# A hybrid decoder layer on one Trainium2 core: the openings of its two feed-forward layers put in the order of the block products, and part of the weight split given to GpSimd

## What is computed

```python
def rmsnorm(x, g):
    xf = x.astype(jnp.float32)
    y = xf * lax.rsqrt(jnp.mean(xf * xf, axis=-1, keepdims=True) + EPS)
    return (y * g.astype(jnp.float32)).astype(x.dtype)

def swiglu(x, w_gate, w_up, w_down):
    return (jax.nn.silu(x @ w_gate) * (x @ w_up)) @ w_down

# in trunk_layer
x = x + 0.5 * swiglu(rmsnorm(x, p['g_ffn1']), p['w1_gate'], p['w1_up'], p['w1_down'])
...
x = x + 0.5 * swiglu(rmsnorm(x, p['g_ffn2']), p['w2_gate'], p['w2_up'], p['w2_down'])
```

## Time and profile before

| | us |
|---|---|
| median of 3 runs | 2257.41 |
| the runs | 2261.75, 2255.10, 2257.41 |
| profiled execution, its own time | 2258.11 |
| its span, first to last instruction | 2256.3 |
| TensorE busy | 2173.1 |
| VectorE busy | 1346.7 |
| ScalarE busy | 712.2 |
| GpSimd busy | 399.7 |
| mean granted clock of TensorE, share of full speed | 0.986 |

### The profile page before, as it was taken

One profiled execution on the slowest core, in us unless ns is written; L12 is line 12 of the kernel. 1 busy time (PEld: TensorE's weight loads), 2 busy tenths in 40 slices (PEclk: granted clock), 3 DMA queues, 4 the chain that ended last, 5 costly groups with the idle time before them and its releaser, 6 DMA issues.

```text
span 2256.3 us, 37791 instructions
## 1 busy us (share of the span) xinstructions
PE 2173.1 (96%) x15020; PEld 2024.1 (90%) x15020; DVE 1346.7 (60%) x2013; ACT 712.2 (32%) x1270; POOL 399.7 (18%) x427
## 2 busy tenths in 40 slices
PE   6799999999999999989999999998999999999998
PEld 5799999998989888878898878988999999989897
DVE  7867666664424678899525145358676676644234
ACT  6422322322212415547312034144223223222122
POOL 1000000000000156768634321520000000000003
PEclk9899999999999999999999999999999999999999
DMA  3122112116423211153411162311221221163222
GB/s 138 60 74 95 60 72 95 65 59 236 120 68 91 99 65 38 59 147 101 166 33 35 37 235 82 134 39 58 77 94 58 76 95 59 66 236 120 68 73 79
DMA packets 70861, 206.63 MB, mean 92 GB/s; under 512 B 9703, under 2 KB 31207, under 8 KB 63079
## 3 DMA queue, kind: packets, MB, share of 16 engines
q1 hardware_dynamic: 67808, 201.84, 26.5%
q10 hardware_dynamic: 2951, 3.35, 0.4%
HBM read 161.14 MB, written 41.23 MB: 90 GB/s over the span
## 4 chain that ended last, share of the span: by engine, by line
PE 85%; DVE 9%; DMA 2%; issue 1%; ACT 1%; POOL 1%; SPq 0%; DVEq 0%; ACTq 0%; POOLq 0%
PE ps L799 27%; PE ps L800 26%; PE ps L801 26%; PE ps L1344 1%; PE ps L1385 1%; DMA dn_raw<-in_w_dn 1%; DVE act_lo L1953 1%; DVE x L2001 1%; DVE t_lo L2009 1%; PE ps L1069 1%; DVE rstd L1940 1%; DMA w_raw<-in_w_plain 0%; DVE acc L2170 0%; PE ps L825 0%; DVE st L2426 0%
## 5 line engine op out<-in xcount | busy, mean ns | idle before, releaser
L799 PE MATMUL ps<-act_hi,op_hi 128*128 128x272 f32 x1280 | 369.8, 289 | 11.4 <-DVE op_lo L2030 11.4
L800 PE MATMUL ps<-act_lo,op_hi 128*128 128x272 f32 x1280 | 371.4, 290 | 0.0
L801 PE MATMUL ps<-act_hi,op_lo 128*128 128x272 f32 x1280 | 370.6, 290 | 0.0
L699 POOL TENSOR_TENSOR w_hi<-w_raw,ones 128x256 fp32r<-128x256 f32 x148 | 133.7, 903 | 1052.8 <-DMA w_raw<-in_w_plain 794.8
L799 PE MATMUL ps<-act_hi,w_hi 128*128 128x288 f32 (+1 forms) x864 | 291.1, 337 | 8.9 <-DVE act_lo L1953 4.4
L799 PE MATMUL ps<-hs_hi,dn_hi 128*128 128x288 f32 (+1 forms) x864 | 284.4, 329 | 0.9 <-DVE x L2129 0.8
L801 PE MATMUL ps<-act_hi,w_lo 128*128 128x288 f32 (+1 forms) x864 | 284.7, 329 | 0.0
L800 PE MATMUL ps<-hs_lo,dn_hi 128*128 128x288 f32 (+1 forms) x864 | 282.4, 327 | 0.0
L801 PE MATMUL ps<-hs_hi,dn_lo 128*128 128x288 f32 (+1 forms) x864 | 282.3, 327 | 0.0
L799 PE MATMUL ps<-t_hi,op_hi 128*128 128x272 f32 x960 | 277.0, 289 | 0.0
L801 PE MATMUL ps<-t_hi,op_lo 128*128 128x272 f32 x960 | 277.0, 289 | 0.0
(11 more groups left out here) (332 smaller groups left out, 4230.2 us busy)
## 6 DMA issues: line engine op xcount, KB each, us to landing
raw_gu<-in_w_gu SPq DMA_DIRECT2D x40, 1024.0 KB, 5.2
...
```

What stands on the lines that cost most here:

```text
L699: steps.done(pool.tensor_tensor(hi[:, r, :], raw[:, r, :], one, ALU.mult))
L799: pe.matmul(out, wh, ah, start=(first and n == 0), stop=False, skip_group_check=goes_on)
L800: pe.matmul(out, wh, al, start=False, stop=False, skip_group_check=goes_on)
L801: ins = pe.matmul(out, wl, ah, start=False, stop=end, skip_group_check=goes_on)
```

## The change

Four things are done, in both layers alike:

- **GpSimd** makes the low parts of tile 1's weights (`second_lo`), in pieces of 128x256, four for gate and four for up, right behind `split_first`. `conv_lo` is gone from VectorE.
- **ScalarE** converts both high parts of tile 1 together, ahead of the squares (first layer) or the square roots (second); it takes gains and silus of tile 0 in turn; and it copies p1 (`keep_p1`) for Quad(0) behind `quad_hi` of steps 4 and 5, ahead of the high part of t4 and of `quad_hi` of step 6.
- **VectorE** evicts the up chunks of tile 0 between the differences of x and no longer behind them; it makes the low parts in the order of the steps that read them, t2, t1, act, t4; the last differences of x, the low parts of act and t4 come behind all evictions and behind `quad_lo` of step 3; U2 (`keep_u2`) is taken for Quad(0) ahead of t4's low part.
- **TensorE** waits for t_lo 2 ahead of step 1 (t2 is first now) and for t_lo 4 ahead of step 3.

The diff, cut to its core:

```diff
+    def second_lo(f):
+        for i, k in enumerate(("gate1", "up1")):
+            pool.wait_ge(f["cv_hi"], upto(f, "cv_hi", i + 1))
+            for r in range(0, KT, SHORT):
+                ins = pool.tensor_tensor(c_lo[k][:, r:r + SHORT, :], raw_gu[i][:, 1, r:r + SHORT, :],
+                                         c_hi[k][:, r:r + SHORT, :].bitcast(F32), ALU.subtract)
+            ins.then_inc(f["cv_lo"], 1)
...
     split_first(f)
+    second_lo(f)
...
             elif j == 1:
                 read(U3, True)
                 if first:
-                    pe.wait_ge(f["t_lo"], upto(f, "t_lo", 4))
+                    pe.wait_ge(f["t_lo"], upto(f, "t_lo", 2))
                     pe.wait_ge(f["up_ev"], upto(f, "up_ev", NC + 1))
...
                 if first:
                     pe.wait_ge(f["up_ev"], upto(f, "up_ev", 2 * NC))
+                    pe.wait_ge(f["t_lo"], upto(f, "t_lo", 4))
...
+    def keep_p1(f, u):
+        act.wait_ge(f["quad_mm"], u.count(STEPS, upto(f, "quad_mm", 1)))
+        if u.later():
+            act.wait_ge(f["quad_ev"], u.count(EVICTS, upto(f, "quad_ev", U3 - EVICTS)))
+        act.activation(p1[:, :, :], ps[:, 0:2, 0:TQ], ACT.Copy).then_inc(f["p1_kept"], 1)
...
         for j in range(STEPS):
             act.wait_ge(f["quad_mm"], u.count(STEPS, upto(f, "quad_mm", j + 1)))
-            if j == 0:
-                if u.later():
-                    act.wait_ge(f["quad_ev"], u.count(EVICTS, upto(f, "quad_ev", U3 - EVICTS)))
-                act.activation(p1[:, :, :], ps[:, 0:2, 0:TQ], ACT.Copy).then_inc(f["p1_kept"], 1)
+            if j == 0 and u.later():
+                keep_p1(f, u)
...
     def ffn_layer(f, gain, kept=None):
-        conv_hi(f, "up1")
         if kept:
-            silu(f, 0, 0)
             act.wait_ge(x_kept, kept)
-        gained(f, gain, range(KT))
-        for c in range(1 if kept else 0, NC):
+        for c in range(NC):
+            gained(f, gain, range(2 * c, 2 * c + 2))
             silu(f, 0, c)
+        gained(f, gain, range(2 * NC, KT))
         act.wait_ge(f["t_sum"], upto(f, "t_sum", 2))
         moving_hi(f, lambda a: t1_hi[:, a:a + 2, :], 0, 0)
         act.wait_ge(f["t_sum"], upto(f, "t_sum", 6))
@@ -1561,18 +1576,19 @@
         moving_hi(f, lambda a: t2_hi[:, a:a + 2, :], KH, TH)
         for j in range(2):
             quad_hi(f, Quad(0), 0, j)
-        for c in range(NC):
-            silu(f, 1, c)
         act.wait_ge(f["gate_mm"], upto(f, "gate_mm", 2 * NC))
         for j in range(2, 4):
             quad_hi(f, Quad(0), 0, j)
+        for c in range(NC):
+            silu(f, 1, c)
         act.wait_ge(f["up_mm"], upto(f, "up_mm", 2 * NC))
         moving_hi(f, lambda a: act_hi[:, a:a + 2, TH:T], 0, TH)
+        for j in range(4, 6):
+            quad_hi(f, Quad(0), 0, j)
+        keep_p1(f, Quad(0))
         act.wait_ge(f["t_sum"], upto(f, "t_sum", 8))
         act.wait_ge(f["hid_out"], upto(f, "hid_out", 32))
         moving_hi(f, lambda a: t4_hi[:, a:a + 2, :], 0, 0)
-        for j in range(4, 6):
-            quad_hi(f, Quad(0), 0, j)
         act.wait_ge(f["t_lo"], upto(f, "t_lo", 8))
         quad_hi(f, Quad(0), 0, 6)
         quad(f, Quad(0), 0)
...
     conv_hi(ffn["ffn1"], "gate1")
+    conv_hi(ffn["ffn1"], "up1")
     for c in range(NC):
...
     conv_hi(ffn["ffn2"], "gate1")
+    conv_hi(ffn["ffn2"], "up1")
     rms("ffn2")
...
-    def conv_lo(f, k):
-        i = int(k == "up1")
-        dve.wait_ge(f["cv_hi"], upto(f, "cv_hi", i + 1))
-        dve.tensor_tensor(c_lo[k][:, :, :], raw_gu[i][:, 1, :, :], c_hi[k][:, :, :].bitcast(F32), ALU.subtract)\
-           .then_inc(f["cv_lo"], 1)
...
+    def keep_u2(f, u):
+        dve.wait_ge(f["quad_mm"], u.count(STEPS, upto(f, "quad_mm", 2)))
+        dve.wait_ge(f["p1_kept"], u.count(1, upto(f, "p1_kept", 1)))
+        if u.later():
+            dve.wait_ge(f["quad_ev"], u.count(EVICTS, upto(f, "quad_ev", 0)))
+        dve.tensor_tensor(u2[:, :, :], ps[:, 2:4, 0:TQ], p1[:, :, :], ALU.add).then_inc(f["quad_ev"], 1)
...
         quad_lo(f, u, s, 6)
         if prepare:
             quad_sums(f, n, 1 - s)
-        made(1)
-        dve.wait_ge(f["p1_kept"], u.count(1, upto(f, "p1_kept", 1)))
         if u.later():
-            dve.wait_ge(f["quad_ev"], u.count(EVICTS, upto(f, "quad_ev", 0)))
-        dve.tensor_tensor(u2[:, :, :], ps[:, 2:4, 0:TQ], p1[:, :, :], ALU.add).then_inc(f["quad_ev"], 1)
+            keep_u2(f, u)
         low(0)
...
     def ffn_layer(f, key):
         for c in range(NC):
             inverse_rms(key, then=lambda c: gate_first(f, c), which=[c])
-        conv_lo(f, "up1")
+        ffn_up(f, 0, 0)
         dve.wait_ge(f["xg"], upto(f, "xg", KH))
         moving_sum(f, 0, 0, 0, TH, 0, 0)
+        ffn_up(f, 0, 1)
         dve.wait_ge(f["xg"], upto(f, "xg", KT))
         dve.wait_ge(f["t_sum"], upto(f, "t_sum", 2))
         moving_sum(f, 0, TH, KH, TH, 0, TH)
         moving_sum(f, KH, TH, KH, TH, 0, 0)
-        for c in range(NC):
-            ffn_up(f, 0, c)
+        ffn_up(f, 0, 2)
         quad_sums(f, Quad(0), 0)
-        moving_lo(f, 0, lambda a: t1_hi[:, a:a + 2, :], lambda a: t1_lo[:, a:a + 2, :], 0, 0)
         for c in range(NC):
             ffn_gate(f, 1, c)
-        moving_lo(f, 2, lambda a: t2_hi[:, a:a + 2, :], lambda a: t2_lo[:, a:a + 2, :], KH, TH)
         for j in range(2):
             quad_lo(f, Quad(0), 0, j)
+        moving_lo(f, 2, lambda a: t2_hi[:, a:a + 2, :], lambda a: t2_lo[:, a:a + 2, :], KH, TH)
         ffn_up(f, 1, 0)
-        for j in range(2, 4):
-            quad_lo(f, Quad(0), 0, j)
+        quad_lo(f, Quad(0), 0, 2)
+        moving_lo(f, 0, lambda a: t1_hi[:, a:a + 2, :], lambda a: t1_lo[:, a:a + 2, :], 0, 0)
         for c in range(1, NC):
             ffn_up(f, 1, c)
+        quad_lo(f, Quad(0), 0, 3)
         dve.wait_ge(f["t_sum"], upto(f, "t_sum", 6))
-        dve.wait_ge(f["t_lo"], upto(f, "t_lo", 2))
+        dve.wait_ge(f["t_lo"], upto(f, "t_lo", 4))
         moving_sum(f, 0, 0, KH, 0, KH, TH)
         moving_lo(f, 4, lambda a: act_hi[:, a:a + 2, TH:T], lambda a: act_lo[:, a:a + 2, TH:T], 0, TH)
+        quad_lo(f, Quad(0), 0, 4)
+        keep_u2(f, Quad(0))
         dve.wait_ge(f["t_sum"], upto(f, "t_sum", 8))
         moving_lo(f, 6, lambda a: t4_hi[:, a:a + 2, :], lambda a: t4_lo[:, a:a + 2, :], 0, 0)
-        for j in range(4, 6):
-            quad_lo(f, Quad(0), 0, j)
+        quad_lo(f, Quad(0), 0, 5)
         quad(f, Quad(0), 0)
...
             gate_out(ffn["ffn1"], c - 1)
-    conv_lo(ffn["ffn1"], "gate1")
     mean_squares("ffn1", D, which=[0, 1])
...
     lo_parts("ffn2", x_tile, "g_ffn2", [2])
-    conv_lo(ffn["ffn2"], "gate1")
     for c in range(NC):
```

1 line of the change is left out of this document (added).

## The result

The changed kernel took 2247.69 us in the median (2245.38 to 2248.75, six runs), the kernel before 2258.45 us in the same session (2255.10 to 2261.75, six runs). The ratio is 0.995 with a 95% interval of 0.9937 to 0.9963: 10.8 us faster by the medians. The profiled execution took 2248.75 us. The forecast was 2246.0, within 2240 to 2252.

The account below looks back on a forecast made before the run. TensorE, busy 96%, can win only its waits, in two openings that VectorE ends. First layer 4.6 plus second 7.8 less 0.7 given back gains 11.7 us from 2258.1: forecast 2246.0, range 2240 to 2252.

Parts of the forecast that it names:

- Evictions early gain nothing, the early copy gains all: Openings: early up-tile evictions remove 9.8 us of waits but only lengthen the next wait, for the p1 copy.
- The p1 copy: Before the third product: six VectorE instructions move behind the copy's release, -7.21 us per layer; one more ScalarE instruction, +0.54.
- Low parts off VectorE: Moving tile 1's low parts to GpSimd saves VectorE 2.27 us in the first layer, 1.13 in the second.
- The price of contention in the first layer: GpSimd's eight pieces hold up VectorE by 0.534 us each, 4.3 us; bounds 0 and 5.9.
- The expected picture: First layer: last chunk's `act_lo` at 0.9 to 1.0 us apiece beside GpSimd's pieces, sqrt chain 3 us later.
- no wait between VectorE and GpSimd: Rival, chance 0.15: the pieces cost VectorE nothing in the first layer, 4.3 us less, total 2241.7.
- a piece dearer than its own length: Rival, chance 0.12: each piece costs VectorE 1.2 us, 9.6 in all; first layer loses 0.7, total 2251.
- Third product: Its start: 86.4 in the first layer (before 90.97), 1546.8 in the second; stops before it 5.3 and 2.8 us.
- Given back: Seventh product waits for C22 behind the moved instructions: about 0.3 us in the first layer, 0.4 in the second.
- The lag heals: In the loop VectorE catches up after the openings; the opposing rival, chance 0.03, loses 14 us, total 2260.
- The sum: Both openings: 4.6 us from the first layer, 7.8 from the second, less 0.7 given back; gain 11.7 us.
- The clock outside the openings: TensorE's granted clock: any change of its slow stretches was taken as 0.

Follow-up runs that it names:

- e7: Changed kernel with the three up-tile evictions of tile 0 back behind the six subtractions of x; 2249.56 us, ratio 0.9954 to the kernel before.
- e8: Changed kernel with the first unit's p1 and U2 copies back at their old places; 2260.61 us, ratio 1.0009 to the kernel before.
- e1: Changed kernel with the low parts of tile 1's weights back on VectorE; 2245.51 us, ratio 0.9941 to the kernel before.
- e4: Changed kernel with GpSimd's first-layer pieces held until the first square root is done; 2245.17 us, ratio 0.9942 to the kernel before.
- e5: Changed kernel with the first unit's p1 copy ahead of the high parts of steps 4 and 5; 2249.41 us.
- e3: Changed kernel with GpSimd's eight pieces per layer made two instructions of 128x1024; 2248.39 us, ratio 0.9956 to the kernel before.
- e6: Changed kernel with the second layer's three reciprocals and first two scalings ahead of the last gate chunk's copy; 2243.28 us.
- best1: Changed kernel with both e4's later pieces and e6's earlier reciprocals; 2241.52 us, ratio 0.9924 to the kernel before.
- best3: best2 with e5's earlier p1 copy added; 2235.57 us, ratio 0.9898 to the kernel before.
- e2: Kernel before with only the GpSimd part (eight pieces, both high parts early on ScalarE); 2259.90 us, ratio 1.0004 to the kernel before.
- best2: best1 with the first unit's step 3 low part behind the evictions of U3 and C22; 2236.62 us, ratio 0.9903 to the kernel before.

## Why the prediction was right, and where its terms were off

The time (2247.69 against 2246.0), the sign and the mechanism held. That the time came as near as 1.7 us is in part luck: the openings won more than forecast (13.4 us for 11.7), and 3.7 us that the sum did not have were lost outside them. Step by step:

- **Evictions early gain nothing, the early copy gains all**: e7 and e8 show it. The early evictions win 0.5 to 0.7 us per layer, a little more than nothing.
- **The p1 copy**, -7.21 + 0.54 per layer: undoing it cost 7.15 us at the third product of the first layer (91.72 for 84.57) and 7.28 in the second (39.80 for 32.52), for 6.67 forecast. The surplus is the low part of step 4 shown under e8, 0.60 us, which the kernel before did not have ahead of its copy: 6.67 + 0.60 = 7.27. U2 is no part of it, since in e8 it starts behind the copy. In the changed kernel the copy starts behind the two `op_hi`, the first of which S, the rewriting of `sums`, releases. ScalarE's timeline of the changed kernel:

```profile
82.76 0.63 ACT L1505 ACTIVATE op_hi<-sums 128x512 fp32r<-128x512 f32 x1 [7.70 <-DVE sums L2050]
...
83.82 0.60 ACT L1520 ACTIVATE p<-ps 128x544 f32<-128x544 f32 x1
```

- **Low parts off VectorE**, 2.27 and 1.13 us: e1 measured 1.12 in the second layer; in the first the 2.27 cannot be told apart from the contention.
- **The price of contention in the first layer, 8 x 0.534 = 4.3 us, was the term that was mis-sized**: it measured 2.7 us (chain of squares) and 2.8 (e1), 0.34 us a piece. The expected picture was wrong as well: `act_lo` was to take 0.9 to 1.0 us apiece and took 0.43, and the loss fell on the squares, at 0.35 us an addition. The first mean of squares came 1.6 us late, for 3.2. The rival "no wait between VectorE and GpSimd" falls too: e4, with the pieces elsewhere, won 2.6 us. The rival of a piece dearer than its own length falls too: at 1.2 us a piece the first layer would have lost, and it won. In the second layer the pieces did slow `act_lo`, eight in 5.93 us for 3.51 before, ahead of an idle of 7.08, so hidden, as said. VectorE there:

```profile
1498.02 5.93 DVE L1971 SCALAR_TENSOR_TENSOR act_lo<-x,cst,act_hi 128x288 fp32r<-128x288 f32 x8
...
1511.99 0.46 DVE L2002 COPY gate_t<-ps 128x288 f32<-128x288 f32 x1 [7.08 <-PE ps L812]
```

- **Third product**: forecast 86.4 in the first layer, measured 84.57, a gain of 6.4 for 4.6; with 2.7 in place of 4.3 for the contention the sum gives 6.2. In the second layer 8.0 for 7.8. The stops before it, 6.01 and 2.46 us, were forecast at 5.3 and 2.8.
- **Given back, 0.7 us**: TensorE's waits for C22 are 1.23 and 1.12. From the third to the seventh product it took 14.93 us in both layers, for 14.45 and 14.34 before, so 0.48 and 0.59 were given back, 1.07 together. The waits are longer than what was given back because the third product itself ran faster: 4.51 us at a granted clock of 0.65 (84.57 to 89.08) for 5.41 at 0.52 (90.97 to 96.38), and TensorE then stood longer for C22, as the prediction said of the clock. e5 shows that VectorE's chain sets where the seventh starts.
- **The lag heals**: no wait for `sg` stands later than the two of the openings in the list of waits.
- **The sum**: forecast 4.3 and 7.4 at the seventh products, measured 5.92 and 7.44. That would be 13.4 us in place of 11.7, and the kernel gained 10.8 by the medians, 9.7 by the spans.
- **The clock outside the openings, taken as 0, is the other term that was off.** Between the seventh product and the second layer's gate tile the changed kernel's profiled execution took 2.5 us longer (1415.49 for 1412.97). TensorE had 37.5 us there at a granted clock of 0.50, before 30.7; 6.8 us more at half speed are up to 3.4 us of work, enough for the 2.5. From the seventh product of the second layer to the end it took 1.1 longer (684.18 for 683.04), which this does not explain: both executions have only the slow stretch at the very end there. The largest single loss shows in the windows (length, busy of PE, PEld, DVE, ACT, POOL, granted clock), in the changed kernel and then at the same stage before:

```profile
1074.00:1091.00 17.00, 15.07 (x66) 11.82 (x67) 3.61 (x3) 3.15 (x5) 16.19 (x20) 0.70 0.19 50
```

```profile
1077.00:1094.00 17.00, 14.64 (x90) 10.14 (x88) 7.14 (x7) 6.99 (x15) 16.37 (x18) 1.00 0.25 70
```

At a granted clock of 0.70 part of the stretch ran at 1.2 GHz, where before all of it had 2.4. Nothing in this stage was changed but when it starts. A slow stretch at this stage stands in the traces of e3, e4, e6, e7, best1 and best3 too, and in none of e1, e2, e5, e8 and best2. Whether the change brings it, or it falls so in one execution and otherwise in another, one trace of each kernel does not settle: e1 to e8 had from 46 to 75 us at the lower clock in all (before 66.4, the change 58.6), with no order that follows the edits.
